# Six units before the second tile is turned, and three low parts on GpSimd

## The reference, cut to what matters

```
h = rmsnorm_2(x, g_pre[l, 0]) * (1 + sc1) + sh1
x = x + 0.5 * gt1 * rmsnorm_2(swiglu_2(h, w_gu1[l], w_dn1[l]), g_post[l, 0])
h = rmsnorm_2(x, g_pre[l, 1]) * (1 + sc2) + sh2
y = token_mixer(h, w_in[l], ...)
x = x + gt2 * rmsnorm_2(y, g_post[l, 1])
h = rmsnorm_2(x, g_pre[l, 2]) * (1 + sc3) + sh3
x = x + 0.5 * gt3 * rmsnorm_2(swiglu_2(h, w_gu2[l], w_dn2[l]), g_post[l, 2])
```

## Time and profile before

| | |
|---|---|
| three runs | 1327.28, 1328.68, 1329.45 us (median 1328.68) |
| the profiled execution | 1332.02 us |
| its span | 1330.2 us |
| PE busy | 1313.2 us (99%) |
| DVE, ACT, POOL busy | 947.5 (71%), 746.0 (56%), 67.1 us (5%) |
| HBM read | 268.66 MB, 203 GB/s over the span |

### The profile page before, as it was taken

How to read it: one execution, slowest core, us unless ns; L and a number is a source line. 1 busy time by engine, 2 the same in 40 slices (tenths; PEclk the granted TensorE clock), 3 DMA queues, 4 the chain that set the end, 5 groups by cost and what they waited for, 6 DMA issues and landing times.

```text
span 1330.2 us, 17136 instructions
## 1 busy us (share of the span) xinstructions
PE 1313.2 (99%) x6371; PEld 1095.7 (82%) x6371; DVE 947.5 (71%) x1352; ACT 746.0 (56%) x1149; POOL 67.1 (5%) x132
## 2 busy tenths in 40 slices
PE   9999999999999999999999999999999999999998
PEld 6888888888887888888788888889988888788886
DVE  6778877856656768887777887677876455766554
ACT  6454457567763644537744435766557663845452
POOL 3100100000000000010000010100000000000000
PEclk9999999999999999999999999999999999999999
DMA  9999966543374699895589996655554355567763
GB/s 288 316 295 310 316 216 193 172 119 104 98 251 159 202 293 304 298 344 162 168 253 297 290 314 199 204 166 175 174 143 113 109 173 170 163 207 215 219 197 105
DMA packets 185491, 282.45 MB, mean 212 GB/s; under 512 B 20386, under 2 KB 133258, under 8 KB 185408
## 3 DMA queue, kind: packets, MB, share of 16 engines
q1 hardware_dynamic: 172672, 238.22, 57.8%
q0 software_dynamic: 12576, 43.06, 9.7%
q10 hardware_dynamic: 160, 0.07, 0.0%
HBM read 268.66 MB, written 1.05 MB: 203 GB/s over the span
## 4 chain that ended last, share of the span: by engine, by line
PE 93%; DVE 3%; ACT 2%; DMA 1%; issue 0%; SPq 0%; DVEq 0%; POOL 0%; ACTq 0%
PE ps L2066 25%; PE ps L2031 16%; PE ps L2033 16%; PE ps L2032 16%; PE ps L2249 2%; PE ps L2045 1%; PE ps L2046 1%; PE ps L2047 1%; PE ps L2149 1%; PE ps L2151 1%; PE ps L2150 1%; PE ps L2081 1%; PE ps L2170 1%; PE ps L2324 1%; PE ps L2308 1%; PE ps L2287 1%
## 5 line engine op out<-in xcount | busy, mean ns | idle before, releaser
L1194 DVE TENSOR_TENSOR w_lo<-raw,w_hi 128x1024 fp32r<-128x1024 f32 (+2 forms) x431 | 513.6, 1213 | 217.4 <-ACT w_hi L676 215.5
L676 ACT ACTIVATE w_hi<-raw 128x1024 fp32r<-128x1024 f32 (+2 forms) x431 | 448.4, 1055 | 367.0 <-DMA raw<-in_ffn_wgu_dram 103.1
L2031 PE MATMUL ps<-w_hi,a_hi 128*128 128x512 f32 (+1 forms) x976 | 386.4, 396 | 1.3 <-DVE w_lo L1194 1.0
L2033 PE MATMUL ps<-w_hi,a_lo 128*128 128x512 f32 (+1 forms) x976 | 378.7, 388 | 0.0
L2032 PE MATMUL ps<-w_lo,a_hi 128*128 128x512 f32 (+1 forms) x976 | 378.2, 387 | 0.0
L2033 PEld LDWEIGHTS ps<-w_hi,a_lo 128*128 128x128 f32 x976 | 183.3, 188 | 38.2
L2031 PEld LDWEIGHTS ps<-w_hi,a_hi 128*128 128x128 f32 x976 | 183.5, 188 | 37.5 <-DVE w_lo L1194 1.5
L2032 PEld LDWEIGHTS ps<-w_lo,a_hi 128*128 128x128 f32 x976 | 183.6, 188 | 35.5
L2066 PE MATMUL ps<-w_hi,hid_hi 128*128 128x512 f32 x300 | 93.1, 391 | 0.0
L2066 PE MATMUL ps<-w_lo,hid_hi 128*128 128x512 f32 x300 | 92.4, 389 | 0.0
L2066 PE MATMUL ps<-w_hi,hid_lo 128*128 128x512 f32 x300 | 92.4, 389 | 0.0
(11 more groups left out here) (438 smaller groups left out, 1600.3 us busy)
## 6 DMA issues: line engine op xcount, KB each, us to landing
raw<-in_ffn_wgu_dram SPq DMA_DIRECT2D x176, 256.0 KB, 4.6
raw<-in_w_in_dram SPq DMA_DIRECT2D x88, 512.0 KB, 3.7
raw<-in_w_gu_dram SPq DMA_DIRECT2D x176, 256.0 KB, 3.7
ada<-in_w_ada_dram POOLq DMA_DIRECT2D x72, 512.0 KB, 6.3
raw<-in_ffn_wdown_dram SPq DMA_DIRECT2D x44, 512.0 KB, 6.0
raw<-in_w_dn_dram SPq DMA_DIRECT2D x44, 512.0 KB, 4.5
raw<-in_w_in_dram SPq DMA_DIRECT2D x36, 256.0 KB, 3.1
raw<-in_w_out_dram SPq DMA_DIRECT2D x16, 512.0 KB, 3.9
```

Of the source, the lines that this page charges most:

```text
L676: act.activation(w_hi[:, u % RING, 0:nk * n], raw[:, u % RING, 0:nk * n], ACT.Copy).then_inc(hi_ready, 1)
L1194: dve.tensor_tensor(w_lo[:, u % RING, 0:nk * n], raw[:, u % RING, 0:nk * n], w_hi[:, u % RING, 0:nk * n].bitcast(F32), ALU.subtract).then_ ...
L2031: pe.matmul(dst(t)[:, 0:n], a[0], slot(u, w_hi, kk, n), start=kc == 0, stop=False)
L2033: i = pe.matmul(dst(t)[:, 0:n], a[1], slot(u, w_hi, kk, n), start=False, stop=kc == KC - 1)
```

## The change

1. At `f2` and `f3` the first tile is multiplied with six units (the four of the first block and the first two of the second block, which go to the second accumulator) before the second tile; the second tile is turned before the sixth of them. The second block's loop then starts at its third unit.
2. At `mix2` the first tile is multiplied with all four units, the second tile is turned, and the narrow unit is multiplied for the first tile; then the four units and the narrow unit for the second tile. The narrow unit so becomes two times 24 matmuls of 128 columns, in two banks, with two copies by ACT, and a count more in `FIRST_TILE`.
3. One unit's low part at each boundary is made by POOL, ahead of its copies of `shift`: unit `up + 2` at `f2`, M2 + 3 at `mix2`, `up + 3` at `f3`. DVE skips it and waits for it before the next unit's low part.
4. The order on DVE and ACT: the second chunk's low part comes ahead of the root `post_root(prev, 1)`; the low parts (and on ACT the high parts) of the fifth and sixth unit come in at new places.

```
+            def unit_lo(u):
+                pool.wait_ge(hi_ready, u + 1)
+                pool.wait_ge(lo_ready, u)
+                pool.tensor_tensor(w_lo[:, u % RING, :], raw[:, u % RING, :], w_hi[:, u % RING, :].bitcast(F32), ALU.subtract)\
+                    .then_inc(lo_ready, 1)
...
             def tile_hi(key):                                  # POOL
                 g = MODS[key]
+                unit_lo(POOL_UNITS[g])
...
+        POOL_UNITS = (ffn[2][0] + 2, M2 + 3, ffn[3][0] + 3)
...
             def lo_part(u):                                    # DVE
+                if u in POOL_UNITS:
+                    return
+                if u - 1 in POOL_UNITS:
+                    dve.wait_ge(lo_ready, u)
...
                 biased_root(f"{key}_1", ss, 1, 3, biases + 4)  # ACT, post_and_norm
+                w.to(end + 4)
                 tile_hi(key, 1)
...
             norm_root("f2", 1)                                 # ACT, f2
             load_table(ACT.Silu)
+            w.to(u_pg + KC + 4)
             tile_hi("f2", 1)
...
                 chunk_lo(key, 0, 0)                            # DVE, post_and_norm
+                chunk_lo(key, 0, 1)
                 post_root(prev, 1)
-                chunk_lo(key, 0, 1)
...
                 tile_root(key, 1)
+                w.to(end + 3)
                 dve.wait_ge(sem("x_ready"), 4 * NORM[key])
                 normalise(key, 1)
-                w.to(end + 3)
+                w.to(end + 4)
                 chunk_lo(key, 1, 0)
...
             w.to(u_pg + KC + 2)                                # DVE, f2
             tile_lo("f2", 0, 4)
+            w.to(u_pg + KC + 3)
             tile_root("f2", 1)
             dve.wait_ge(sem("x_ready"), 16)
             normalise("f2", 1)
+            w.to(u_pg + KC + 4)
             chunk_lo("f2", 1, 0)
...
-            def first_cols(u0, dst, key, src, turn_at):        # PE
+            def first_cols(u0, dst, key, src, turn_at, n=4, behind_tile=None):
                 for t in range(T):
-                    for i in range(4):
+                    for i in range(n):
                         if t == 0 and i == turn_at:
                             turn_tile(key, src, 1)
...
+                    if t == 0 and turn_at == n:
+                        turn_tile(key, src, 1)
+                    if behind_tile is not None:
+                        behind_tile(t)
...
-                        first_cols(up, lambda t: acc(t, 0), FFN[f], x if f == 1 else h, 2 if f == 1 else 3)
+                        first_cols(up, acc, FFN[f], x if f == 1 else h, 2 if f == 1 else 5, 4 if f == 1 else 6)
                         continue
-                    for i in range(4):
+                    for i in range(2 if f >= 2 and j == 1 else 0, 4):
...
-                    first_cols(u0, lambda t: acc(t, 1), "mix2", h, 3)
+                    first_cols(u0, lambda t, j: acc(t, 1), "mix2", h, 4, behind_tile=lambda t: narrow_unit(u_mix2[0], t))
```

More of the change, by code:

```diff
@@ L293, in acc, with narrow_rows @@
             return ps[:, 2 * t + s, :]
+        def narrow_rows(t):
+            return ps[0:32, 2 if t == 0 else 7, 0:P]
         def turned(m):
@@ L442, in two_blocks @@
         SKEW = 4
-        FIRST_TILE = {"f0": 1, "merge": 2, "wo": 3, "f1": 4, "emb": 5, "f2": 7, "merge2": 9, "mix2": 11, "f3": 13}
+        FIRST_TILE = {"f0": 1, "merge": 2, "wo": 3, "f1": 4, "emb": 5, "f2": 7, "narrow": 9, "merge2": 10, "mix2": 12, "f3": 14}
         def pss_at(key, t, half=1):
@@ L1092, in _ @@
             w.to(M2 + 4)
+            act.wait_ge(sem("first_tile"), FIRST_TILE["narrow"])
+            act.activation(smT[:, 0:P], narrow_rows(0), ACT.Copy).then_inc(sem("mix2_evac"), 1)
             for b in BLOCKS2:
@@ L1102, in _ @@
                     act.wait_ge(used, u1)
-                    act.activation(smT[:, :], ps[0:32, 7, 0:S], ACT.Copy).then_inc(sem("mix2_evac"), 2)
+                    act.activation(smT[:, P:S], narrow_rows(1), ACT.Copy).then_inc(sem("mix2_evac"), 1)
                     w.to(u1 + 4)
@@ L2048, in standing_unit, with narrow_unit @@
                 i.then_inc(used, 1)
-            def narrow_unit(u):
+            def narrow_unit(u, t):
                 pe.wait_ge(lo_ready, u + 1)
-                dst = ps[0:32, 7, 0:S]
+                dst = narrow_rows(t)
+                tile = slice(t * P, (t + 1) * P)
                 for c in range(KC):
                     hi, lo = (slot(u, w_, c, 32) for w_ in (w_hi, w_lo))
[L2056 to L2059, removed]
+                    pe.matmul(dst, hi, a_hi[:, c, tile], start=c == 0, stop=False)
+                    pe.matmul(dst, lo, a_hi[:, c, tile], start=False, stop=False)
+                    i = pe.matmul(dst, hi, a_lo[:, c, tile], start=False, stop=c == KC - 1)
+                if t == 0:
+                    i.then_inc(sem("first_tile"), 1)
+                else:
+                    i.then_inc(used, 1)
             def row_half(u, kc, t, last, hi, lo, bank):
@@ L2136, in first_rows, with first_cols @@
                             i.then_inc(used, 1)
-            def first_cols(u0, dst, key, src, turn_at):
+            def first_cols(u0, dst, key, src, turn_at, n=4, behind_tile=None):
                 for t in range(T):
-                    for i in range(4):
+                    for i in range(n):
                         if t == 0 and i == turn_at:
@@ L2145, in first_cols @@
                         for kk in range(2):
-                            kc = 2 * i + kk
-                            tile_ready(key, t, kc)
+                            kc = 2 * (i % 4) + kk
+                            if i < 4:
+                                tile_ready(key, t, kc)
+                            to = dst(t, i // 4)
                             a = [v[:, kc, t * P:(t + 1) * P] for v in (a_hi, a_lo)]
-                            pe.matmul(dst(t), a[0], slot(u0 + i, w_hi, kk, 512), start=kc == 0, stop=False)
-                            pe.matmul(dst(t), a[0], slot(u0 + i, w_lo, kk, 512), start=False, stop=False)
-                            ins = pe.matmul(dst(t), a[1], slot(u0 + i, w_hi, kk, 512), start=False, stop=kc == KC - 1)
+                            pe.matmul(to, a[0], slot(u0 + i, w_hi, kk, 512), start=kc == 0, stop=False)
+                            pe.matmul(to, a[0], slot(u0 + i, w_lo, kk, 512), start=False, stop=False)
+                            ins = pe.matmul(to, a[1], slot(u0 + i, w_hi, kk, 512), start=False, stop=kc == KC - 1)
                         if t == T - 1:
                             ins.then_inc(used, 1)
+                    if t == 0 and turn_at == n:
+                        turn_tile(key, src, 1)
+                    if behind_tile is not None:
+                        behind_tile(t)
             def turn_tile(key, src, t, c0=0, c1=KC):
@@ L2569, in _ @@
                 if b == 0:
-                    narrow_unit(u0)
                     continue
                 if b == 1:
-                    first_cols(u0, lambda t: acc(t, 1), "mix2", h, 3)
+                    first_cols(u0, lambda t, j: acc(t, 1), "mix2", h, 4, behind_tile=lambda t: narrow_unit(u_mix2[0], t))
                     continue
+                if b == 2:
+                    pe.wait_ge(sem("mix2_evac"), 1)
                 if 9 <= b <= 12:
```

12 lines of the change are left out of this document (10 added, 2 removed).

## The result

Before: 1328.54 us (median of 6 runs, 1327.28 to 1329.45). After: 1333.97 us (6 runs, 1332.73 to 1335.23). Ratio 1.004, 95% interval 1.0029 to 1.005: the change makes the kernel about 5 us slower. In a repetition (last experiment) it was 1.0031 [1.0019, 1.0042]. The profiled execution after took 1333.97 us, its span is 1332.1.

What follows compares the result with a forecast made beforehand. PE, busy 99%, was taken to bound the kernel, so only its waits at the boundaries count. Part 1 +3.4, f3 -0.65, mix2 -0.65, f2 +1.7 gave +3.8 us on 1328.68: 1332.5 us, range 1327.3 to 1338.0.

Steps and rivals of the forecast that it cites:

- part 1: Before the three first turns: POOL's low part (2.0 us) holds DVE operations with two SBUF inputs; sum +3.4 us.
- part 2: From the first turn on at f3 and mix2: the new order removes PE's waits, gaining 0.65 us at each.
- Rival (b): At mix2 the narrow unit isn't cheaper by width (1334.8 us) or falls back to full-precision pace (1341); chance 0.12.
- part 3: From f2's first turn on: unit 4's high part comes only after two table loads, so PE waits; +1.7 us.
- Rival (d): The reading of f2 is wrong, unit 4 is in time, POOL's part short; each boundary gains: 1326.0 us, chance 0.08.
- Rival (c), the clock: PE's clock falls after longer stands before f3's or f2's turns: one fall 1334.2 us, two 1335.9; chance 0.14.

Runs made afterwards that it cites:

- after_again: The changed kernel, unchanged, run once more against the kernel before: 1333.39 us against 1329.28, ratio 1.0031.
- pool_reads_idle: Changed kernel, but DVE makes all low parts and POOL does same-size subtractions of constants into a buffer nobody reads: 1334.58 us against 1328.51, 1.0052.
- f2 alone: The kernel before with only f2's part of the change (six units first, its order on ACT, DVE and PE): 1330.17 us against 1328.51, 1.0015.
- f2 mended and the low part first: Changed kernel without POOL's low parts, f2's high and low parts reordered, next low part before the second root at mix2 and f3: 1325.06 us, 0.9972.
- no_pool_old_f2: Changed kernel without POOL's low parts, with f2 in its old order with four units: 1326.35 us against 1328.40, 0.9986.

## Why the prediction was right

The forecast was +3.8 (1332.5 us), the result +5.3 and +4.1 by the two ratios. Each of the forecast's mechanisms is there; what was off are sizes.

- **POOL's hold (part 1).** Right in kind and place, at all three boundaries, and the main loss. Its size was off: POOL's subtraction takes 2.39 us and not the 2.0 taken between 1.1 and 2.9. So the first turns were put 1.05 to 1.2 us later; they come 1.70 (f2) and 1.60 (mix2) later, and 1.52 at f3 (at the end), 4.8 instead of 3.4. The second error in it is what is given back: 0.37 to 0.47 us per boundary were measured (2.07, 2.07 and 1.99 with DVE's low part left in, against the change), where 0.55 and 0.7 were taken for mix2 and f3. At f2 the size came out and its reason did not. The prediction let the turn wait for ACT's eviction, with 0.5 us in hand. In the kernel before, DVE has no idle time from the held sum to the turn's root, and with its low part left in the whole hold arrives (2.07 of 2.08). Nothing is in hand there; the 0.37 is DVE's low part, taken out of this chain:

```profile
642.98 0.15 DVE L1812 TENSOR_SCALAR root_bias<-first_half 128x1 f32<-128x1 f32 x1
643.16 1.23 DVE L1194 TENSOR_TENSOR w_lo<-raw,w_hi 128x1024 fp32r<-128x1024 f32 x1
644.31 0.15 DVE L1815 SCALAR_TENSOR_TENSOR rt<-ss,root_bias 128x1 f32<-128x1 f32 x1
```

The estimate by the Trainium skill (GPSIMD Engine Reference, "Performance versus the Vector engine"), some 2.2 us, was nearer to the 2.39 than the value taken.
- **From the first turn on, f3 (part 2).** Without POOL: 20.74 us against 21.36, -0.62 for the -0.65 forecast, with PE's waits of 0.20 and 0.51 where 0.4 and 0.6 were put. By the distance of two starts, which is what a wait costs in the stream, they are 0.36 and 0.66, so the terms were right.
- **The same, mix2.** -1.06 for -0.65. The mis-sized terms are the narrow unit, 0.058 to 0.060 us a matmul and not 0.065 (some 0.2 us more in all and not 0.4), and the 0.4 that PE was to wait for h, which isn't there: the second turn starts 8.27 us behind the first, where 8.5 was put. Rival (b) is out.
- **f2 (part 3).** +1.54 in the kernel after from the first turn on, +1.7 forecast, with the named wait behind the second table load (PE 1.17, then 0.24). Rival (d) is out: unit 4 was not in time, and another order on ACT and DVE turns the loss into a gain.
- **Rival (c), the clock.** It did fall, once, at f3, as the rival had it. But its price was read wrongly. From f3's first turn to its second the change takes 10.32 us (1141.80 to 1152.12), the kernel without POOL's low parts 10.16 (1136.52 to 1146.68); the fall costs 0.16 (0.19 in after_again) and not 1.7. In the slow stretch PE runs late, and so does not have to stand 0.20 and 0.51 for DVE. Counted by the distance of starts, these two waits and the slower starts behind them cost 1.2 us in the kernel without POOL's low parts: what the clock took was mostly time that PE would have waited. With the longer stand of 3.27 it does cost: in pool_reads_idle f3's part is +3.0, of which the stand is 2.3.

By the terms as measured the sum is 4.8 - 1.06 - 0.6 + 1.6 = +4.7, and the table of after has +4.8.

## What to carry to other kernels

Before moving work to GpSimd, list which VectorE operations will run beside it. If GpSimd's reads SBUF and VectorE's has two SBUF inputs, add what is left of GpSimd's operation to VectorE's chain (2.0 of 2.39 us here), even where the VectorE step is a single column and even if nobody waits for GpSimd; "GpSimd is idle" isn't an argument. When work is put ahead of a turn (six units for four), follow each new operand back through every engine's queue: at f2 one high part behind a table load made PE wait 1.17 us, and the part lost 1.6. And price a slower clock against the waits that it covers.

## What was not expected

**f3's first turn follows a weight's landing.** It was read as bound by the chain of roots. Here are DVE's timeline ahead of f3's first turn in the kernel before, and ACT's high part for the same unit in the kernels with f2 alone and with f2 mended and the low part first:

```profile
1131.93 1.23 DVE L1194 TENSOR_TENSOR w_lo<-raw,w_hi 128x1024 fp32r<-128x1024 f32 x1 [0.62 <-ACT w_hi L676]
1133.08 0.15 DVE L1239 TENSOR_SCALAR root_bias<-first_half 128x1 f32<-128x1 f32 x1
1133.26 1.29 DVE L1306 TENSOR_TENSOR h<-ps,GT 128x512 f32<-128x512 f32 x2
1134.46 0.15 DVE L1227 SCALAR_TENSOR_TENSOR rt<-pss,root_bias 128x1 f32<-128x1 f32 x1
```

```profile
1128.97 1.06 ACT L676 ACTIVATE w_hi<-raw 128x1024 fp32r<-128x1024 f32 x1 [1.25 <-DMA raw<-in_w_gu_dram]
```

```profile
1124.40 1.06 ACT L688 ACTIVATE w_hi<-raw 128x1024 fp32r<-128x1024 f32 x1 [0.69 <-DMA raw<-in_w_gu_dram]
```

ACT's high part waits for its transfer, DVE's low part for the high part, and the first root stands behind that low part in DVE's queue; from the low part to the turn's root DVE shows no idle time. From the start of that high part to the first turn it is 8.57 us in the first (turn at 1137.54) and 8.57 in the second (1132.97), and 8.56 to 8.58 in five others, the kernel before among them; with POOL's low part it is 10.09 to 10.10 in three. That is how the 1.52 above was got. PE's stand before this turn differs from 0.45 to 1.45 us between kernels that are alike there, by how late the unit lands, and this is the scatter in the table's f3 column. ACT's squares stand behind the same high part, but they don't set the turn: in no_pool_old_f2 the second of them started 1.83 us behind the high part instead of 1.53, since it waited for PE, and the turn came at 8.56 all the same.

```profile
1127.15 0.60 ACT L714 ACTIVATE junk<-ps 128x512 f32<-128x512 f32 x1 [0.20 <-PE ps L2105]
```

So it is DVE's low part that would have to go behind the roots; whether PE would then pay for it was not tried.

**A one-column step can be held for 2 us.** The length of the held operation plays no part: 0.22 us became 2.21, the 0.69 of 512 columns 2.77.
